# Two blocks in one kernel: the order of the first block's projection and mixers, its modulation vectors and its tables are changed

## The reference, cut to what matters

```python
mod = c @ w_ada + b_ada                       # 1024 -> 6 vectors of 1024
sh_m, sc_m, gt_m, sh_f, sc_f, gt_f = split(mod, 6)
h = rms_norm(x, g_pre_mix) * (1 + sc_m) + sh_m
z = h @ w_in                                  # 1024 -> 1280
u, f, q, k, v = split(z)                      # 384, 256, 384, 128, 128
y_ssm = s5_mixer(u, ...)      # 24 groups, 64 complex states, forward and backward scan, then a gate
y_fft = fourier_mixer(f, w_fft)               # 2-d FFT, real part
y_att = window_attention(q, k, v, sink)       # 6 query heads, 2 key heads, blocks of 128, window 128
y = concat([y_ssm, y_fft, y_att]) @ w_out
x = x + gt_m * rms_norm(y, g_post_mix)
h = rms_norm(x, g_pre_ffn) * (1 + sc_f) + sh_f
...                                           # feed-forward part, then the second block
```

```python
scores = q @ k / 8 - slope * dist             # masked outside the window
m = maximum(max(scores), sink)
p = exp(scores - m); p = p / (sum(p) + exp(sink - m))
```

## Time and profile before

| | us |
|---|---|
| median of 3 runs (lowest, highest) | 3353.91 (3346.64, 3356.39) |
| the profiled execution, its whole time | 3354.79 |
| its span, first to last instruction | 3353.0 |

### The profile page before, as it was taken

One profiled execution on the slowest core, in us unless ns is written; L12 is line 12 of the kernel. 1 busy time (PEld: TensorE's weight loads), 2 busy tenths in 40 slices (PEclk: granted clock), 3 DMA queues, 4 the chain that ended last, 5 costly groups with the idle time before them and its releaser, 6 DMA issues.

```text
span 3353.0 us, 31513 instructions
## 1 busy us (share of the span) xinstructions
PE 2930.7 (87%) x12826; PEld 2304.7 (69%) x12826; DVE 1345.2 (40%) x1718; ACT 877.1 (26%) x1273; POOL 857.8 (26%) x434
## 2 busy tenths in 40 slices
PE   4694568879999999969998999886987999999996
PEld 4463445668888888857776887763466888888874
DVE  5977851256453444442224212434724211111115
ACT  2341241332121121222343213331032321211111
POOL 0231201324342333312211221110033433323332
PEclk8897778879999999978999999897987999999997
DMA  5237513121111111202212222213532111111112
GB/s 193 88 128 172 162 54 116 63 82 51 44 50 51 51 44 47 104 13 96 65 57 69 70 81 76 69 63 120 159 113 94 44 44 48 45 47 51 45 59 111
DMA packets 91456, 263.24 MB, mean 79 GB/s; under 512 B 12064, under 2 KB 26928, under 8 KB 91312
## 3 DMA queue, kind: packets, MB, share of 16 engines
q1 hardware_dynamic: 76176, 217.90, 20.0%
q0 software_dynamic: 8032, 26.59, 2.2%
q10 hardware_dynamic: 7104, 16.75, 1.4%
HBM read 211.52 MB, written 49.68 MB: 78 GB/s over the span
## 4 chain that ended last, share of the span: by engine, by line
PE 75%; DVE 12%; ACT 6%; issue 3%; DMA 2%; POOL 1%; SPq 1%; ACTq 0%; POOLq 0%; DVEq 0%
PE ps L1027 21%; PE ps L1028 21%; PE ps L1029 21%; PE pc L1338 3%; DVE tab L1364 3%; PE pss L1293 2%; PE pss L998 2%; DVE acc L1370 1%; ACT L2074 1%; ACT whl L2074 1%; PE ps L1209 1%; ACT sq L2074 1%; ACT E L2074 1%; DVE y L1364 1%; ACT act L2074 1%
## 5 line engine op out<-in xcount | busy, mean ns | idle before, releaser
L2489 POOL TENSOR_TENSOR whl<-wraw,whl 128x1024 fp32r<-128x1024 f32 x228 | 592.7, 2602 | 1725.6 <-ACT whl L2074 1725.6
L1027 PE MATMUL ps<-act,whl 128*128 128x512 f32 x2464 | 998.4, 405 | 40.3 <-POOL whl L2489 15.6
L1028 PE MATMUL ps<-act,whl 128*128 128x512 f32 x2464 | 980.7, 398 | 0.0
L1029 PE MATMUL ps<-act,whl 128*128 128x512 f32 x2464 | 978.4, 397 | 0.0
L1027 PEld LDWEIGHTS ps<-act,whl 128*128 128x128 f32 x2464 | 477.4, 194 | 158.9 <-issue 45.5
L1028 PEld LDWEIGHTS ps<-act,whl 128*128 128x128 f32 x2464 | 476.6, 193 | 102.0 <-issue 4.3
L1029 PEld LDWEIGHTS ps<-act,whl 128*128 128x128 f32 x2464 | 475.5, 193 | 102.8
L1027 PE MATMUL ps<-hid,whl 128*128 128x512 f32 x864 | 349.5, 405 | 12.2 <-issue 7.8
L1028 PE MATMUL ps<-hid,whl 128*128 128x512 f32 x864 | 345.9, 400 | 0.0
L1029 PE MATMUL ps<-hid,whl 128*128 128x512 f32 x864 | 345.6, 400 | 0.0
L2074 ACT ACTIVATE whl<-wraw 128x1024 fp32r<-128x1024 f32 x228 | 239.3, 1052 | 310.8 <-PE ps L1029 303.2
(11 more groups left out here) (274 smaller groups left out, 2785.0 us busy)
## 6 DMA issues: line engine op xcount, KB each, us to landing
wraw<-in_w_in SPq DMA_DIRECT2D x62, 512.0 KB, 4.0
wraw<-in_f1u SPq DMA_DIRECT2D x44, 512.0 KB, 3.3
wraw<-in_f2d SPq DMA_DIRECT2D x36, 512.0 KB, 3.3
wraw<-in_w_out SPq DMA_DIRECT2D x32, 512.0 KB, 3.4
gs<-gt SPq DMA_DIRECT2D x32, 512.0 KB, 4.9
wraw<-in_f2u SPq DMA_DIRECT2D x32, 512.0 KB, 3.3
sgm<-gs SPq DMA_DIRECT2D x30, 512.0 KB, 3.7
uT<-in_w_ada POOLq DMA_DIRECT2D x24, 512.0 KB, 4.7
```

The costliest lines, as they stand in the source:

```text
L1027: pe.matmul(PSB[g.bank][:, :], hi, src[:, 0, k, c], start=e == 0, stop=False)
L1028: pe.matmul(PSB[g.bank][:, :], hi, src[:, 1, k, c], start=False, stop=False)
L1029: m = pe.matmul(PSB[g.bank][:, :], lo, src[:, 0, k, c], start=False, stop=e == len(ks) - 1)
L2489: return g_.tensor_tensor(out, a, b, op)
```

## The change

What it does, part by part:

- **Vectors j = 0, 1 on PE.** No products on DVE: each 128x1024 piece is the stationary operand of 8 matmuls against one column of c, accumulated over k in PSUM. `ada_out` on PE falls away for them.
- **Vectors j = 2 to 5** move from the mixers to `w_out`, into buffers of their own; four steps are put behind each tile of the first half, one behind each of the second, loads on POOL, products on DVE, the sum over the partitions on PE.
- **Tables.** Exponents 16 instead of 31; the product of 720 columns is gone; `tab_ko` takes K from V and b in parts of 112 columns, and adds the diagonal by small matmuls with `Ct`, `Cn` and `dI`, so `tab_kl` and `tab_end` go. `tab_cs` comes between the table groups. V and W tables have two buffers each.
- **Order.** Before `w_in`: 18 steps of tables (instead of 8), so four groups with their matmuls. `fence(0)` is gone. `w_in` has four PSUM banks at first, and its first three panels are taken together, k by k, for each half. A plan time `now` (0.68 us for each k of a tile, other values for PE steps) says when the side generators `tables_left`, `ssm` and `attention` put their steps: within a tile, after any k. Attention begins when panel 3 of `w_in` (the first queries) is done; from then on `w_in` has one PSUM bank, and attention the other three.
- **State space.** `ssm_x(b+1)` comes before `ssm_scan(b)`, `ssm_y(b)` after `ssm_rot(b+1)`.
- **Attention.** The scale of q carries 1/slope, and one `tensor_tensor_reduce` adds the distance, multiplies by the slope and takes the maximum with the sink. The sink's exponential is made on ACT from the sink column; ACT also scales the scores (`att_scale`). The output goes to `qT` and is split into the activations at the end (`att_split`).

```diff
+    def beside(self, gen, after=0.0):
+        self.aside.append([self.now + after, gen])
+    def poll(self):
+        while self.aside:
+            entry = min(self.aside, key=lambda e: e[0])
+            if entry[0] > self.now:
+                break
+            try:
+                entry[0] = self.now + next(entry[1])
+            except StopIteration:
+                self.aside.remove(entry)
+    def mm(self, t, k0, k1):
+        a = k0
+        for k in range(k0, k1):
+            self.now += 0.68
+            if any(at <= self.now for at, _ in self.aside):
+                self.put("mm", t, a, k + 1)
+                a = k + 1
+                self.poll()
+        if a < k1:
+            self.put("mm", t, a, k1)
...
+            elif len(self.banks) == 4:
+                ns = [self.panel(name, i) for i in first]
+                for half in range(2):
+                    pre = [self.tile(kind, i, n, half, True) for i, n in zip(first, ns)]
+                    for k in range(8):
+                        for t in pre:
+                            self.mm(t, k, k + 1)
+                    for i, n, t in zip(first, ns, pre):
+                        self.put("ev", t)
+                        if half:
+                            self.panel_done(n, t)
+                        yield (i, t) if half else None
+                first = ()
...
     def ada(j, n0):
         for k in range(8):
             p.put("ada", j, k, n0 + k)
-            if k % 2:
-                yield
-        yield
-        p.put("ada_out", j, p.hold.get(1) if j >= 2 else None)
-        if j >= 2:
-            p.hold[1] = ("adaD", "mod", j)
+            yield
+        p.put("ada_out", j)
         yield
     def tables():
         p.put("tab_load")
         yield
-        for k in range(6):
+        for k in range(5):
             p.put("tab", k)
             yield
-        for b0 in range(0, NG, GB):
+        for n, b0 in enumerate(range(0, NG, GB)):
             p.put("tab_v", b0)
+            p.put("tab_vst", b0)
             yield
             p.put("tab_w", b0)
             yield
-            p.put("tab_vst", b0)
+            if n < 6:
+                p.put("tab_cs", n)
+                p.put("tab_cst", n)
+                yield
             p.put("tab_k", b0)
-            yield
             p.put("tab_wst", b0)
             p.put("tab_ko", b0)
-            yield
             p.put("tab_kst", b0)
-        p.put("tab_kl")
-        for n in range(6):
-            p.put("tab_cs", n)
-            yield
-            p.put("tab_cst", n)
-        p.put("tab_end")
-        yield
         p.had.add("tables")
...
     p.put("start")
     tab = tables()
-    norm0 = first_norm()
     next(tab)
-    for n, _ in enumerate(norm0):
-        if n % 2:
-            next(tab, None)
-    p.put("fence", 0, False)
+    p.put("x_load")
+    mods = chained(ada(0, 0), ada(1, 8))
+    for j in range(8):
+        next(mods)
+        next(tab)
+        p.put("x_sq", j)
+    for _ in range(3):
+        p.load()
+    for _ in mods:
+        next(tab)
+    p.put("x_rstd")
+    for _ in range(3):
+        p.split()
+    p.banks = (0, 1, 2, 3)
+    for half in range(2):
+        p.put("apply", 0, half)
     p.put("mix_load")
     n_us = [0]
-    def ada_rest():
-        while ("v", 1) not in p.had or n_us[0] < 3:
-            yield
-        for n, j in enumerate((2, 4, 3, 5)):
-            yield from ada(j, 16 + 8 * n)
-        p.had.add("ada_fin")
-    def w_in():
-        for r in p.gemm("w_in", W_IN_ORDER, 3):
-            if r is not None:
-                p.had.add(("z", r[0]))
-                if r[0] < 3:
-                    p.put("u_store", r[0], r[1])
-                    n_us[0] += 1
-            yield
     def ssm():
+        while not made():
+            yield 1.0
         p.put("ssm_load")
-        yield
-        for _ in range(3):
-            yield
+        yield 8.0
+        p.pe(3.6, "ssm_x", 0)
+        p.put("ssm_r", 0)
+        p.put("ssm_rot", 0)
+        yield 5.0
         for b in range(6):
-            p.put("ssm_x", b)
-            yield
-            p.put("ssm_rot", b)
-            yield
+            if b:
+                p.pe(2.7, "ssm_y", b - 1)
+                p.put("ssm_out", b - 1)
+                yield 1.5
+            if b < 5:
+                p.pe(3.6, "ssm_x", b + 1)
             p.put("ssm_scan", b)
-            yield
             p.put("ssm_back", b)
-            for _ in range(4):
-                yield
-            p.put("ssm_y", b)
-            yield
-            p.put("ssm_out", b)
-            yield
+            if b < 5:
+                yield 8.0
+                p.put("ssm_r", b + 1)
+                p.put("ssm_rot", b + 1)
+                yield 5.0
+        yield 9.0
+        p.pe(2.7, "ssm_y", 5)
...
         nu = 24
         for u in range(nu + 3):
+            while u < nu and ("z", 3 + UNITS[u][0]) not in p.had:
+                yield 1.0
             if 0 <= u - 1 < nu:
                 p.put("att_exp", u - 1)
             if u < nu:
+                p.pe(0.8, "att_score", u)
+            if 0 <= u - 2 < nu:
+                p.put("att_scale", u - 2)
             if u >= 3:
+                p.pe(1.3, "att_out", u - 3)
             if 0 <= u - 1 < nu:
                 p.put("att_norm", u - 1)
+            yield 1.2
             if 0 <= u - 2 < nu:
+                p.pe(0.8, "att_t", u - 2)
+            yield 0.8
+        while "w_in" not in p.had:
+            yield 1.0
+        for i in range(3):
+            for half in range(2):
+                p.put("att_split", i, half)
+        p.had.add("att")
...
+    def tables_left():
+        for _ in tab:
+            yield 3.0
+    p.beside(tables_left())
+    p.beside(ssm())
+    for r in p.gemm("w_in", W_IN_ORDER, 3):
+        if r is not None:
+            p.had.add(("z", r[0]))
+            if r[0] < 3:
+                p.put("u_store", r[0], r[1])
+                n_us[0] += 1
+            if r[0] == 3:
+                p.banks = (1,)
+                p.beside(attention())
+    p.had.add("w_in")
+    while "att" not in p.had:
+        p.now = max(p.now, min(e[0] for e in p.aside))
+        p.poll()
+    fourier()
+    p.settle()
...
+                if s == 1:
+                    for _ in range(1 if half else 4):
+                        next(mods, None)
...
+    mods = chained(*(ada(j, 16 + 8 * n) for n, j in enumerate((2, 4, 3, 5))))
...
+            def ada(j, k, n):
+                if j >= 2:
+                    return
+                w.wait_ge(*done("d_par"))
+                w.wait_ge(*done(f"d_as{n % 4}", n))
+                for i in range(8):
+                    m = pe.matmul(PSS[:, j, i:i + 1], ring0[n % 4][:, i * 128:i * 128 + 128], col("c", k),
+                                  start=k == 0 and i == 0, stop=k == 7, skip_group_check=True)
+                m.then_inc(*mark("ada", j, k))
+            def ada_out(j):
+                if j < 2:
+                    return
                 w.wait_ge(*done("adaD", j, 7))
+                w.wait_ge(*done("adaD", "mod", ADA_BEFORE[j]) if j in ADA_BEFORE else done("gluA", "sig", 2, 1))
                 for i in range(8):
+                    m = pe.matmul(PSC[1][:, i:i + 1], acc1[:, i * 128:i * 128 + 128], onesm[:, 0:1], start=True, stop=True)
...
             def tab_ko(b0):
+                at = VAT[b0 // GB % 2]
+                w.wait_ge(*done("tabD", "v", b0))
+                w.wait_ge(*done("tabD", "cn"))
                 w.wait_ge(*done("tabA", "wt", b0, 1))
+                fw, bw = slice(0, 64), slice(64, 128)
                 for g in range(GB):
+                    o0, o1 = (PSC[e][32 * g:32 * g + 16, :] for e in range(2))
                     for i in range(2):
+                        b, q = Bt[:, i, b0 + g, :], at + 384 * i + 128 * g
+                        pe.matmul(o0[:, 0:112], b[bw, :], R[bw, q + 16:q + 128], start=i == 0, stop=i == 1)
+                        pe.matmul(o1[:, 128:240], b[fw, :], R[fw, q:q + 112], start=i == 0, stop=i == 1)
+                for g in range(GB):
+                    o1 = PSC[1][32 * g:32 * g + 16, 112:128]
+                    pe.matmul(o1, Bt[:, 0, b0 + g, :], Ct[:, 0, b0 + g, :], start=True, stop=False)
+                    pe.matmul(o1, Bt[:, 1, b0 + g, :], Cn[:, b0 + g, :], start=False, stop=False)
+                    m = pe.matmul(o1, ident[:, 0:16], dI[:, b0 + g, :], start=False, stop=True)
...
-                    stt(sc[:, g, 0:wd], dist[:, lo:hi], slope, PSS[:, g, 0:wd], ALU.mult, ALU.add).then_inc(
-                        *mark("attD", "bias", u, g))
+                    v.tensor_tensor_reduce(sc[:, g, 0:wd], PSS[:, g, 0:wd], dist[:, lo:hi], slope, col("sink", 2 * i + g),
+                                           ALU.add, ALU.max, sm[:, g:g + 1]).then_inc(*mark("attD", "bias", u, g))
                 w.wait_ge(*done("attD", "bias", u, 1))
-                v.tensor_reduce(sm[:, 0:2], sc[:, :, 0:wd], AX.X, ALU.max).then_inc(*step("attD"))
```

(13 more changed lines are left out.)

438 lines of the change are left out of this document (181 added, 257 removed).

## The result

The changed kernel takes 3382.84 us (median of 4 runs, 3379.39 to 3384.52) against 3350.27 of the kernel before: a ratio of 1.0094, 95% interval 1.0074 to 1.0115, so 33 us slower. The forecast was 3333, range 3275 to 3378.

A forecast was written before the change was run, and what follows sets the result against it. TensorE was taken as not the limit while the first block is mixed (VectorE busy 38.7 of 40 us early), but full in w_out. Start +46, middle -88, w_out +21 gave -21 us: 3333 us, range 3275 to 3378.

The forecast's parts named there:

- the start: Up to the first matmul of w_in: 46 us longer, PE's queue full at the slow clock, first matmul at 140 us.
- +21 us: w_out: four sums, 7 us, plus three PE waits of about 5 us in its first half, 14; bounds 8 and 30.
- 468 becomes 380: Middle, first matmul of w_in to first of w_out: 297 us of PE work plus 83 of stalls, 88 us less.
- behind `apply` (17): Head of w_in: PE waits 17 us at tab_k(12) for a table product that DVE has behind both halves of apply.
- the DMAs of U and its weights (22): Middle: ssm_x(0) waits 22 us for U, whose DMAs and weights land late.
- the single bank (10): Middle, once attention begins: w_in's last 8 tiles each wait for ACT to empty the one bank, 10 us in all.
- The 14 us for scan and back: Middle: PE waits for DVE's ssm_scan and ssm_back, 3.5 us a block on four blocks of six.
- my signs of being wrong: First matmul before 120 us, middle waits for DVE over 65 us, or ACT, not PE, the chain's engine in the last units.
- The 20 us for the last units: Middle, after w_in is used up: 20 us of stall over some 9 attention passes that only ACT, DVE and gate fill.
- rival 1: The start runs at 2.4 GHz: first matmul at about 92 us, 48 us less, 3285 us; chance 13%.
- rival 2: Middle: the interleaving hides the 34 us of uncertain stalls, 3299 us; chance 18%.
- Rival 3: PE's single queue: chain waits block the projection too; 80 us stay, middle 426 us, whole 3379 us; chance 16%.

The follow-up runs named there:

- late sums: Changed kernel with TensorE's sums of the four vectors one tile later, and two products a tile instead of one in the second half: ratio 1.0017 to the kernel before.
- e7_scale_dve: Changed kernel with the scaling of the attention scores back on VectorE instead of ScalarE: ratio 1.0055 to the kernel before.
- e6_serial: Changed kernel with all 20 tiles of w_in ahead of the state-space part and attention, not interleaved with them: ratio 1.0040 to the kernel before.
- e2_ada_mid: Changed kernel with the other four modulation vectors moved from w_out to the middle, behind the last state-space block: ratio 1.0006 to the kernel before.
- e10_fast_tables: Changed kernel with first two vectors on VectorE, late sums, all tables behind w_in's first tiles; against that kernel (3286.01 us), table groups closer: 3290.04 us, 0.9816.
- e9_wide_sq: Changed kernel with x's sums of squares by 16 matmuls of 512 columns instead of 128 of one, without diagonal and broadcast: ratio 1.0084 to the kernel before.

## Why the prediction was wrong

Two steps failed, by 30 us each, and the start, 17 us better than forecast, hid a part of that.

**`w_out` is the first step that failed.** It was put at "+21 us", "Bounds 8 and 30", and was 51.2. The place (three waits for DVE's `acc` in half 0, the fourth sum without one) was right, the size was not: "PE waits about 5 us. That occurs three times" against 14.19, 7.89 and 9.27. I followed the last load, through POOL's queue, and gave the product 1.3 us at its end; I did not list what stands in front of it on VectorE: the norm addition of PE's own last tile and up to four products, one of which takes 3.2 us in place of 1.28 where it meets POOL's split. The late sums take 29 us out of half 0, which shows that order for the second and third wait; x's loads account for 8 of the first. The 51 in sum: waits 31.4, three sums at the slow clock 3 x 3.58 = 10.7, tiles slowed by the clock about 6 (PE is busy with its 216 tile instructions for 57.5 us there against 51.7), 2.9 more for the root (7.42 against 4.54). I had counted 7 us of sums at the fast clock and left the restarts to the bounds.

**The start** was "+46", first tile at 140; it was +28.7 and 122.7. The mechanism held: PE's queue full from 16.1 to 112 us (93.5 busy) at weight loads of 333 ns for the one-column matmuls, and 10.7 us behind it. Mis-sized was above all `tab_ko`, "I take 4.5", which took 1.35 (72.79 to 74.14), and the wait before it, 0.58 for 1.1; so a table group took 3.45 us, not 7.1: 14.6 us of the 17. The other 3 are instructions that overlap at their ends, 3.41 us for 16 in place of 3.58.

**The middle is the second**: it was "468 becomes 380", and became 411.2. Near what was written: 14.7 us behind `apply` (17), 14.8 and 1.8 for the DMAs of U and its weights (22), about 5.5 for the single bank (10). The 14 us for scan and back were 25.4, in two forms: 10.7 of `ssm_y` waiting, and 14.7 of attention scores waiting for VectorE, which itself waits in two of these three cases for the reload of `Cb` (5.21 and 3.54 us). The sentence that failed is "ACT takes over the scaling ...; I cost that at nothing": it is the engine of the last units, 3.70 us each in place of 2.73, and e7_scale_dve, which moves the scaling back, shortens the middle by 10.4 us. That was also one of my signs of being wrong. The 20 us for the last units took it that `w_in` is used up by then; in the trace its last four tiles stand behind attention (438.9 to 463.3) and none lies between those units. PE stands still for 112.9 us of the middle, 18 more than the 83 and the 12 that were in the 55 at its end; the other 13 us I put down to the slow clock (0.88), which no run tried. And e6_serial shows that the interleaving, which I took for the source of the gain, cost about 13 us. So the 57 us come from the rest of the change. VectorE's busy time in the middle falls from 326.6 to 170.7 us, but a good part of that work, four groups of tables and 32 products, only moved to the start and to `w_out`; e2_ada_mid prices the four vectors at 26 us, and how the remainder divides no run shows.

**The rivals.** The start did not run fast (rival 1), and nothing was hidden better than forecast (rival 2). Rival 3 names a time near the one measured, 3379, but its price, 80 us of waits kept in the middle, is not what decided: the middle was still 57 us shorter. That the time is near its 3379 is chance. The slower kernel came from a term that I had in the sum at less than half its size, with no rival for it, and from a middle that gained two thirds of what I had put down.

## What to carry to other kernels

When a step is moved beside a stream of tiles, list for each engine what stands in front of it, and ask whether anything there waits for the waiting engine's own last result; if so the consumer belongs one tile later, which here gave back 26 us (1.0094 to 1.0017). When loads and other work share an in-order queue, ask also what waits behind the loads: here POOL's split of the next weights did, for 8.8 us of PE. Look at what will be left behind the last chain with nothing beside it: starting the state-space part 63 us sooner (e10_fast_tables) moved nothing, since 102 us of such work stood at the end. An engine that is busy four tenths of the time (ScalarE, 157.5 us of 411) is free only where the chain in question does not run through it back to back.

## What the runs showed of the hardware

- PE issued one-column matmuls, with four groups of table matmuls between them, for 96 us and was busy for 93.5 of them. The weight loads of the one-column matmuls took 333 ns throughout, the duration at 1.2 GHz (the earlier trace rows has 192 ns at the other level), while the clock column of the same stretch reads 1.00 (first the loads: least, median, most in ns; then the stretch). The trace has no clock record before 120.3 us, and the column counts such time as full speed, so here the loads tell the level and the column does not. In e9_wide_sq, whose records begin at 23.6 us, the column (1.00 to 30.5, then 0.50) and the loads agree.

```profile
L1097 PEld LDWEIGHTS pss<-par,adaw x256: 288/333/338, 16.0 to 108.1; 128*128 128x128 f32 x128
```

```profile
16.00:112.00 96.00, 93.54 (x576) 90.31 (x576) 46.73 (x106) 31.90 (x66) 13.17 (x21) 1.00 0.44 160
```

The Trainium skill ("TensorE: Matmul & The Clock Gate", Part 1) says that activity releases the throttled clock; this stream keeps PE busy for 97% of the time and ran at the slow level to its end, and with wide matmuls mixed in (e9_wide_sq) it ran at the fast level for 6.9 and 3.4 us only.

- VectorE's norm addition and POOL's split held each other up: the addition takes 0.69 us by itself (579.26) and 2.83 us where it meets POOL's split (587.18 beside 586.72 above), ending 0.55 us behind it; of the four products at 579.88, the one that meets the split at 580.33 takes 3.23 us and the others 1.28. The split takes 2.4 us alone (544.59) and 2.7 to 3.1 there. The Trainium skill ("SBUF — State Buffer", "Who interferes with whom") says that VectorE with two inputs in SBUF and a GpSimd operation that reads SBUF exclude each other for a whole instruction; the rows agree with that.
